# A hybrid decoder layer on one core: fp32 side products spread between dense passes, and an opening loaded and ordered differently

## The reference

```python
xn = rms_norm(h, pre_norm[i])
proj = xn @ w_in[i]
(g_q, g_k, g_v, g_a, g_z, n_q, n_kc, n_vc, n_ks, n_vs, n_kw, n_vw, n_g, n_z) = \
    jnp.split(proj, SPLIT_POINTS, axis=-1)
log_a = jax.nn.log_sigmoid((g_a @ gla_a_up[i] + gla_a_bias[i]).astype(jnp.float32)) / GLA_TAU
o_gla = gla_mixer(g_q..., g_k..., g_v..., log_a...)
...
    flat = blocks.transpose(0, 1, 3, 2, 4).reshape(B, n_cmp, NSA_KV_HEADS, CMP_LEN * NSA_DH)
    return jax.nn.silu(flat @ w1) @ w2        # compressed keys and values of the NSA
...
mixed = jnp.concatenate([o_gla, o_nsa], axis=-1) @ w_out[i]
h = h + rms_norm(mixed, post_norm[i])
```

## Time and profile before

| | us |
|---|---|
| median of 3 runs | 894.94 |
| lowest, highest | 894.93, 896.84 |
| the profiled execution | 893.85 |
| its span, first to last instruction | 892.1 |

### The profile page before, as it was taken

The page is one execution under the profiler, slowest core; times in us unless marked ns, Lnnn a source line. Parts: engine busy times, 40 slices in busy tenths (PEclk is TensorE's granted clock), DMA queues, the critical chain, the costliest instruction groups (busy, mean ns, idle before and its releaser), DMA issues.

```text
span 892.1 us, 12441 instructions
## 1 busy us (share of the span) xinstructions
PE 840.9 (94%) x4624; PEld 693.7 (78%) x4624; DVE 538.1 (60%) x953; ACT 460.3 (52%) x928; POOL 374.0 (42%) x331
## 2 busy tenths in 40 slices
PE   6999999999999999988889998999989999999996
PEld 6878798888888788766667776777767888887884
DVE  2670449761744504666989998899966026372445
ACT  4513134223222026666879988789966252625424
POOL 3312028244221121643447655356534445463554
PEclk9999879999999999998999999999999999999999
DMA  8511011111011021310000000000007723232237
GB/s 253 134 51 48 23 33 48 48 32 52 25 48 36 24 50 49 100 36 1 1 1 1 1 1 2 1 1 1 1 1 255 240 83 98 70 110 75 98 95 247
DMA packets 38398, 55.19 MB, mean 62 GB/s; under 512 B 11313, under 2 KB 17729, under 8 KB 38338
## 3 DMA queue, kind: packets, MB, share of 16 engines
q1 hardware_dynamic: 38050, 53.35, 19.7%
q0 software_dynamic: 288, 1.05, 0.7%
HBM read 49.13 MB, written 5.25 MB: 61 GB/s over the span
## 4 chain that ended last, share of the span: by engine, by line
PE 74%; DVE 11%; ACT 10%; issue 3%; POOL 1%; DMA 0%; DVEq 0%; SPq 0%; ACTq 0%; POOLq 0%
PE psum L863 45%; PE psum L1102 3%; ACT pT_hi L1442 3%; DVE pT_lo L2042 3%; PE psum L952 3%; PE psum L1119 3%; ACT p_win L1428 2%; PE psum L1120 2%; PE psum L1086 2%; PE psum L896 2%; PE psum L1087 1%; PE psum L802 1%; PE psum L804 1%; PE psum L803 1%; DVE p_slc L2016 1%
## 5 line engine op out<-in xcount | busy, mean ns | idle before, releaser
L1563 POOL TENSOR_TENSOR w_lo<-w_raw,w_hi 128x512 fp32r<-128x512 f32 x126 | 179.9, 1431 | 353.4 <-ACT w_hi L1224 353.0
L1224 ACT ACTIVATE w_hi<-w_raw 128x512 fp32r<-128x512 f32 x126 | 79.3, 635 | 309.6 <-PE psum L863 301.3
L2042 DVE TENSOR_TENSOR pT_lo<-psum,pT_hi 128x512 fp32r<-128x512 f32 (+1 forms) x148 | 100.0, 684 | 17.2 <-ACT pT_hi L1442 16.2
L1442 ACT ACTIVATE pT_hi<-psum 128x512 fp32r<-128x512 f32 (+1 forms) x148 | 86.8, 592 | 31.8 <-PE psum L1102 30.8
L863 PE MATMUL psum<-w_hi,xT_hi 128*128 128x512 f32 x256 | 101.2, 395 | 1.7 <-DVE gla_state_b L1923 1.7
L863 PE MATMUL psum<-w_lo,xT_hi 128*128 128x512 f32 x256 | 100.1, 391 | 0.0
L863 PE MATMUL psum<-w_hi,xT_lo 128*128 128x512 f32 x256 | 100.1, 391 | 0.0
L1119 PE MATMUL psum<-pT_hi,v_hi_lo 128*128 128x512 f32 x132 | 60.9, 461 | 17.3 <-DVE pT_lo L2042 17.1
L1086 PE MATMUL psum<-kT_hi_hi,qT_hi_lo 128*128 128x384 f32 (+3 forms) x192 | 70.4, 370 | 4.3 <-DVE neg_max L2016 4.0
L1619 POOL TENSOR_SCALAR p_slc<-p_slc,gate_over_sum 128x512 f32<-128x512 f32 (+7 forms) x40 | 63.7, 1604 | 1.6
L1428 ACT ACTIVATE p_slc<-p_slc,neg_max 128x512 f32<-128x512 f32 (+7 forms) x80 | 58.1, 727 | 7.5 <-DVE neg_max L2016 7.3
(11 more groups left out here) (276 smaller groups left out, 2020.1 us busy)
## 6 DMA issues: line engine op xcount, KB each, us to landing
w_raw<-in_w_in SPq DMA_DIRECT2D x56, 256.0 KB, 2.7
w_raw<-in_w_out SPq DMA_DIRECT2D x32, 256.0 KB, 2.8
w_raw<-in_ple_gate SPq DMA_DIRECT2D x32, 256.0 KB, 2.6
x_tok<-in_x SPq DMA_DIRECT2D x8, 512.0 KB, 4.7
h_tok<-in_x SPq DMA_DIRECT2D x8, 512.0 KB, 5.0
out<-h_tok SPq DMA_DIRECT2D x6, 512.0 KB, 5.6
w_raw<-in_ple_proj SPq DMA_DIRECT2D x8, 256.0 KB, 2.5
rank_w_raw<-in_w_in SPq DMA_DIRECT2D x8, 128.0 KB, 2.8
```

The source lines that it names most:

```text
L1224: act.activation(w_hi(i)[:, 0:w], w_in(i)[:, 0:w], ACT.Copy).then_inc(s_whi, 1)
L1442: act.activation(PTh[0:n, u % 4], bank(4 + u % TRING)[0:n], ACT.Copy).then_inc(s_phi, 1)
L1563: pool.tensor_tensor(w_lo(i)[:, 0:w], w_in(i)[:, 0:w], w_hi(i)[:, 0:w].bitcast(F32), ALU.subtract).then_inc(s_wlo, 1)
L2042: dve.tensor_tensor(PTl[0:n, u % 4], bank(4 + u % TRING)[0:n], PTh[0:n, u % 4].bitcast(F32), ALU.subtract).then_inc(s_plo, 1)
```

## The change

It does six things. (1) PE runs four fp32 products of 256 columns on constants before the first transposes and three behind them (`keep_busy`); nobody reads them. (2) ACT loads its function table with a tiny copy right after the constants. (3) The rank weights come in nine transfers (slice 0, slices 1 to 3, slices 4 to 7), all ahead of tiles 2 to 7 of x; the rank-up weights and bias follow x. (4) In group 0 the transposes of tiles 2 and 3 stand behind slices 4, 5, 6 and 7. (5) Two of the four rank-up products run inside group 2, behind its slice 6, the other two between hidden products 6 and 12. (6) The diagonals stream 64 columns (the same two, repeated) and stand, with the compression's output, between the banks of the first pass of `gv`, whose bank order is 0, 1, 2, 3, 6, 4, 5, 7. DVE and the waits follow suit.

```diff
 CUTS = ((0, 48), (48, 176), (176, 304))
+LOADS = ((0, 1), (1, 4), (4, 8))
 LEVELS = (2, 4, 8, 16, 32, 64, 128)
...
         if i < KD:
-            eng.wait_ge(s_ag[i], 48)
+            eng.wait_ge(s_ag[[lo <= i < hi for lo, hi in LOADS].index(True)], 48)
         else:
...
-        def load_rank_piece(k):
-            rows, dst, w = slice(k * P, (k + 1) * P), AGR[:, k], a["w_in"][0]
-            sp.dma_start(dst[:, 0:32], w[rows, NG_:NG_ + 32]).then_inc(s_ag[k], 16)
-            sp.dma_start(dst[:, 32:48], w[rows, GA:GA + RANK]).then_inc(s_ag[k], 16)
-            sp.dma_start(dst[:, 48:304], w[rows, NKC:NKC + 256]).then_inc(s_ag[k], 16)
+        def load_rank_pieces(n):
+            lo, hi = LOADS[n]
+            rows, w = slice(lo * P, hi * P), a["w_in"][0]
+            for at, col, size in ((0, NG_, 32), (32, GA, RANK), (48, NKC, 256)):
+                sp.dma_start(AGR[:, lo:hi, at:at + size],
+                             w[rows, col:col + size].rearrange("(k p) c -> p k c", p=P)).then_inc(s_ag[n], 16)
...
         load_x(1)
-        for k in range(3):
-            load_rank_piece(k)
-        load_x(2)
-        load_x(3)
-        for k in range(3, KD):
-            load_rank_piece(k)
-        for t in range(4, NT):
+        for n in range(len(LOADS)):
+            load_rank_pieces(n)
+        for t in range(2, NT):
             load_x(t)
+        sp.dma_start(GAU[32:32 + RANK, :], a["gla_a_up"][0]).then_inc(s_gau, 16)
+        sp.dma_start(GBI[:], a["gla_a_bias"][0].rearrange("(c p) -> p c", p=P),
+                     allow_slow_non_contiguous=True).then_inc(s_gau, 16)
         for i in range(KD, KD + RAW):
...
                          allow_slow_non_contiguous=True).then_inc(s_small, 16)
-        sp.dma_start(GAU[32:32 + RANK, :], a["gla_a_up"][0]).then_inc(s_small, 16)
-        sp.dma_start(GBI[:], a["gla_a_bias"][0].rearrange("(c p) -> p c", p=P),
-                     allow_slow_non_contiguous=True).then_inc(s_small, 16)
         sp.dma_start(GGN[:], a["gla_out_norm"][0].partition_broadcast(P)).then_inc(s_small, 16)
...
+        def rank_up(half, ct):
+
+            pe.matmul(bank(2 * half + ct), GAU[32:32 + RANK, ct * P:(ct + 1) * P],
+                      AG[32:32 + RANK, half * 512:half * 512 + 512],
+                      start=True, stop=True).then_inc(s_la, 1)
+
+        def keep_busy(n):
+
+            for _ in range(n):
+                pe.matmul(bank(0)[:, 0:256], ident, CT[:, 0:256], start=True, stop=True)
+
+        keep_busy(4)
         for t in range(2):
...
                     mm.then_inc(s_xtr, 1)
+        keep_busy(3)
         for k in range(KD):
             project_rank(0, k)
-            if 2 <= k < 6:
-                turn_x(4 + k - 2)
+            if k >= 4:
+                turn_x(k)
         for k in range(KD):
...
                               DR[:, half].rearrange("p t j -> p (t j)"), start=True, stop=True).then_inc(s_rrow, 1)
-
-        def project(name, tokens, ready=None, begin=0):
+            if k == 6:
+                pe.wait_ge(s_gau, 32)
+                for ct in range(2):
+                    wait_read(pe, cidx["ag"], ct)
+                    rank_up(0, ct)
+
+        def project(name, tokens, ready=None, begin=0, first_order=None, between={}):
...
                     if first:
-                        b = (b + begin) % banks
+                        b = first_order[b] if first_order else (b + begin) % banks
                     if first and ready:
...
                         mm.then_inc(s_bank, 1)
+                    if first and b in between:
+                        between[b]()
                 if not final:
...
                 pe.wait_ge(s_rt, b - 5)
+            elif b < 2:
+                pe.wait_ge(s_z, b + 1)
             else:
...
-
-        pe.wait_ge(s_small, 16 * 39)
-        for ct in range(2):
-            for half in range(2):
-                wait_read(pe, cidx["gqk"], ct * 2 + half)
-                pe.matmul(bank(ct * 2 + half), GAU[32:32 + RANK, ct * P:(ct + 1) * P],
-                          AG[32:32 + RANK, half * 512:half * 512 + 512],
-                          start=True, stop=True).then_inc(s_la, 1)
+        def hidden(n, l):
+
+            flat = DC[:, n].rearrange("p c t -> p (c t)")
+            blocks = flat[:, 2 * l:2 * l + CSTR * (CROWS - 1) + 1:CSTR]
+            return pe.matmul(bank(4 + n)[:, 0:CROWS], W1[:, n, l], blocks, start=(l == 0), stop=(l == 15))
+
+        def diagonal(t):
+
+            if t == 0:
+                pe.wait_ge(s_cbr, 1)
+                pe.wait_ge(s_prod, 1)
+            for ct in range(2):
+                at = t * GH + 2 * ct
+                mm = pe.matmul(bank(7)[:, at:at + 64], QKP[:, ct, t * P:(t + 1) * P],
+                               CT[:, C_HEAD:C_HEAD + 2].unsqueeze(1).to_broadcast([P, 32, 2]), start=True, stop=True)
+            if t == NT - 1:
+                mm.then_inc(s_diag, 1)
+
+        def compressed():
+
+            pe.wait_ge(s_ch, 1)
+            for n in range(2):
+                for kv in range(NKV):
+                    mm = pe.matmul(bank(4 + n)[0:NCMP, kv * DH:(kv + 1) * DH], HCT[:, n, kv * 64:kv * 64 + NCMP],
+                                   W2[:, n], start=True, stop=True)
+            mm.then_inc(s_cout, 1)
+
+
+        pe.wait_ge(s_small, 16 * 37)
         pe.wait_ge(s_dcs, 2)
-        for n in range(2):
-            wait_read(pe, cidx["gqk"], 4 + n)
-            for l in range(16):
-
-                flat = DC[:, n].rearrange("p c t -> p (c t)")
-                blocks = flat[:, 2 * l:2 * l + CSTR * (CROWS - 1) + 1:CSTR]
-                mm = pe.matmul(bank(4 + n)[:, 0:CROWS], W1[:, n, l], blocks, start=(l == 0), stop=(l == 15))
+        wait_read(pe, cidx["gqk"], 4)
+        for l in range(16):
+            hidden(0, l)
+            if l in (5, 11):
+                wait_read(pe, cidx["gqk"], 2 + l // 11)
+                rank_up(1, l // 11)
+        wait_read(pe, cidx["gqk"], 7)
+        for l in range(16):
+            mm = hidden(1, l)
+            if l == 2:
+                pe.wait_ge(s_pws, 2)
+                for n in range(2):
+                    m1 = pe.matmul(bank(7)[:, n:n + 1], PS_[:, n], CT[:, C_ONE:C_ONE + 1], start=True, stop=True)
+                m1.then_inc(s_cb, 1)
         mm.then_inc(s_cmp, 1)
-        wait_read(pe, cidx["gqk"], 7)
-        pe.wait_ge(s_pws, 2)
-        for n in range(2):
-            mm = pe.matmul(bank(7)[:, n:n + 1], PS_[:, n], CT[:, C_ONE:C_ONE + 1], start=True, stop=True)
-        mm.then_inc(s_cb, 1)
-        wait_read(pe, cidx["gqk"], 6)
         pe.wait_ge(s_agg, 1)
...
         mm.then_inc(s_gtr, 1)
-        pe.wait_ge(s_cbr, 1)
-        pe.wait_ge(s_prod, 1)
-        for t in range(NT):
-            for ct in range(2):
-                mm = pe.matmul(bank(7)[:, t * GH + 2 * ct:t * GH + 2 * ct + 2], QKP[:, ct, t * P:(t + 1) * P],
-                               CT[:, C_HEAD:C_HEAD + 2], start=True, stop=True)
-        mm.then_inc(s_diag, 1)
-        pe.wait_ge(s_ch, 1)
-        for n in range(2):
-            for kv in range(NKV):
-                mm = pe.matmul(bank(4 + n)[0:NCMP, kv * DH:(kv + 1) * DH], HCT[:, n, kv * 64:kv * 64 + NCMP], W2[:, n],
-                               start=True, stop=True)
-        mm.then_inc(s_cout, 1)
...
-            if b < 4:
-                pe.wait_ge(s_z, 4)
+            if b < 2:
+                wait_read(pe, cidx["gqk"], b)
+            elif b < 4:
+                pe.wait_ge(s_z, b + 1)
             elif b < 6:
...
                 pe.wait_ge(s_dg, 1)
+
+        def diagonals(b):
+            def some():
+                for t in {0: (0,), 1: (1,), 2: (2,), 3: (3, 4), 6: (5, 6, 7)}[b]:
+                    diagonal(t)
+                if b == 2:
+                    compressed()
+            return some
...
-        project("gv", xt, after_compression)
+        project("gv", xt, after_compression, first_order=(0, 1, 2, 3, 6, 4, 5, 7),
+                between={b: diagonals(b) for b in (0, 1, 2, 3, 6)})
         for lev in (0, 1, 2):
...
         act.wait_ge(s_const, 32)
+        act.activation(first_table[:], CT[:, C_ONE:C_ONE + 2], ACT.Copy)
...
-        def read_out(c):
+        def read_out(c, banks=None):
             name = chunks[c][0]
-            for b in range(chunks[c][3]):
+            for b in banks or range(chunks[c][3]):
                 ps, done = bank(b), bank0[c] + b + 1
...
-        def raise_rank(ct):
-
-            for half in range(2):
-                dve.wait_ge(s_la, 2 * ct + half + 1)
-                dve.tensor_scalar(GLZ[:, ct, half * 512:half * 512 + 512], bank(2 * ct + half),
+        def raise_rank(half):
+
+            for ct in range(2):
+                dve.wait_ge(s_la, 2 * half + ct + 1)
+                dve.tensor_scalar(GLZ[:, ct, half * 512:half * 512 + 512], bank(2 * half + ct),
                                   GBI[:, ct:ct + 1], None, ALU.add).then_inc(s_z, 1)
...
         dve.wait_ge(s_xtr, 2 * KD)
-        read_out(cidx["ag"])
```

(6 more changed lines are left out.)

4 lines of the change are left out of this document (3 added, 1 removed).

## The result

The changed kernel takes 900.32 us (median of 5 runs, 899.01 to 901.10); the kernel before took 894.93 beside it (892.90 to 896.84). The ratio is 1.006 with an interval of 1.0042 to 1.0078: slower by 0.6%. The forecast was 902.2 within 897.6 to 906.5, slower. The profiled execution took 901.1 us with a span of 899.3; before, and all others come from a span of 892.1.

What follows compares the result with a forecast made beforehand. PE was taken to bound the kernel. Group 1 5.8 us later (pauses 7.2 less slow clock 1.4), plus 3.0 for the clock, less 1.5 for the stage, gives +7.3 on 894.94: 902.2 us, range 897.6 to 906.5.

Steps and rivals of the forecast that it cites:

- first product: Start of group 0: first rank product at 11.5 us against 11.46, between 10.7 and 12.3; start and table load cancel.
- slow clock of the first slices: Group 0: the first slices run at 2.4 GHz instead of about 1.2, which gives back 1.4 us.
- three pauses: Group 0: PE stands 2.40 us before each of slices 5, 6 and 7, waiting for ACT and POOL; 7.2 us.
- clock in the pauses: Group 0 into group 1: PE's clock falls in the pauses and costs 3.0 us, between 0 and 4.5.
- stage behind gqk: Between gqk and gv: gains 2.9 us, less 1.0 for a new wait and 0.4 for product changes; 1.5 us net.
- The two cases: Start: first product at 12.0 or 12.3 us with transposes at 1.2 GHz, 10.7 or 10.4 with the clock up.
- a diagonal's price: Between gqk and gv: 0.21 us per diagonal is its weight load; 64 columns hide under it, higher clock gains nothing.
- Rival D: Not slower: clock at 2.4 GHz through gv's first pass, early start, stage gives its full 2.9 us; 897.1 us, chance 0.11.
- much more than 3 us: Sign that the prediction is wrong: the stage behind gqk gives back much more than 3 us.
- A: The forecast: three pauses in group 0, clock falls in them, short products keep it up later; 902.2 us, chance 0.52.
- B: The pauses in group 0 come, but the clock outlasts them; 899.2 us, chance 0.22.
- C: The clock falls a second time, in gv's first pass, which runs partly slow; 905.3 us, chance 0.15.

Runs made afterwards that it cites:

- as_is: The changed kernel once more, unedited, for a second profile: 900.14 us, ratio 1.0062.
- act_order: The changed kernel with ACT making the high parts of slices 4 to 7 before it takes up transpose units 4 to 7: 892.78 us, ratio 0.998.
- turns_back: The changed kernel with the transposes of tiles 2 and 3 put back behind slices 2 to 5 of group 0: 890.58 us, ratio 0.9971.
- turns_only: The kernel before with only the transposes of tiles 2 and 3 moved behind slices 4 to 7 of group 0: 906.1 us, ratio 1.0135.
- filled: The changed kernel with four constant fp32 products of 256 columns put into each of the three pauses: 899.91 us, ratio 1.006.
- no_busy: `act_order` without the seven constant products, early table load kept: 892.81 us, ratio 0.9984.
- early_diag: `act_order` with the diagonals moved ahead, two token tiles behind each of banks 0 to 3: 891.83 us, ratio 0.9963.
- best: `early_diag` with three constant products ahead of the transposes and two behind, instead of four and three: 890.39 us, ratio 0.9954.
- block64: The kernel before with diagonals streaming 64 columns instead of 2, in the old single block: 893.98 us, ratio 0.9989.
- before_again: The kernel before once more, unedited, for a second profile: 895.2 us, ratio 1.0016.
- cols2: `act_order` with diagonals of 2 columns instead of 64, at the same spread places: 892.03 us, ratio 0.9973.
- stage_only: The changed kernel with the opening of the kernel before, so only the stage between gqk and gv stays changed: 893.48 us, ratio 0.9997.

## Why the prediction was right, and where it was not

The time was 1.9 us from the forecast (+5.4 against +7.3), the sign and the chief cause were right. By its own sum, for the two profiles of the changed kernel (the price of the slow clock at the start is what is left over in the column of `as_is`; the prices of the fall and of the stage are worked out above):

| term | forecast | first profile | `as_is` |
|---|---|---|---|
| first product | 0 | −0.9 | −0.4 |
| slow clock of the first slices | −1.4 | −1.4 | −1.4 |
| three pauses | +7.2 | +7.3 | +7.3 |
| clock in the pauses | +3.0 | +2.0 | 0 |
| stage behind gqk | −1.5 | −3.7 | −2.3 |
| attention stages | 0 | +3.9 | +1.8 |
| sum | +7.3 | +7.2 | +5.0 |

**The pauses** were the step that decides, and every part of it held: the place, the chain of ACT and POOL, 2.40 us forecast and 2.43 measured for each, 7.3 in all. `act_order` and `turns_back` take them away in two different ways, and by the ratios 7 to 8 us go with them (1.006 becomes 0.998 and 0.9971); `turns_only` brings them into the kernel before alone. `filled` confirms the sum to 0.1 us where the clock has no part: −0.93 − 1.4 + 7.3 = 4.97, and group 2 stood at +4.95.

**The clock in the pauses** was mis-sized: 2.0 us where it falls, not 3.0, and it doesn't always fall. The rule of the Trainium skill (TensorE: Matmul & The Clock Gate, Why this matters for your kernels) that pauses between bursts have to be longer than these before they matter would have excluded it. One profile agrees with the rule and one doesn't: in the first it fell at 23.9 us, at the beginning of the third pause of 2.18 us.

**The start.** My value was 11.5 us, between 10.7 and 12.3; 10.52 and 11.04 were measured, and 10.46 to 11.25 in the experiments with all seven constant products, so the early bound was too late as well. Sixteen transposes took some 2 us, not 3.65, because the constant products had brought the clock up by 6.8 to 8.1 us. The two cases had been written down; the choice of the middle was the error. That the constant products would also hide a late tile of x wasn't seen. Slice 0 at 1.09 us confirms the clock's part, and `no_busy`, 1.6 us later than `act_order` at group 2 with the same first product, is near its 1.4; on the median it doesn't show.

**The stage behind gqk** is where a step failed. The prediction held that a diagonal's price is its weight load of 0.206 us "although the clock was low", so that "the higher clock gains nothing". It took 0.21 us from the timeline at 1.2 GHz and 0.206 from the record of another line's weight loads at 2.4 GHz, and called them one. The weight loads of the diagonals themselves would have told: in the kernel before they are 333 ns long at 1.2 GHz, at a distance of 0.21, so the record's length isn't the distance and goes with the clock. So would the block's own first matmuls, 0.11 us apart at 116.56 and 116.67 us, ahead of the fall.

```profile
L912 PEld LDWEIGHTS psum<-consts,gla_qk_products x23: 333/333/333, 117.2 to 121.9; 128*128 128x128 f32 x23
```

The same line after, 128.2 to 130.9 us, with the clock at 2.4 GHz, min, median and max in ns:

```profile
L916 PEld LDWEIGHTS psum<-consts,gla_qk_products x19: 187/192/192, 128.2 to 130.9; 128*128 128x128 f32 x19
```

The diagonals and the compression's output took 124.13 − 116.43 = 7.70 us before and 4.85 after with the wait in it, so a gain of 2.85 where −1.0 was forecast (0 for them and the wait of 1.0, which was 0.79). The other terms were smaller than forecast: the dense products of `gv`'s first pass gained 0.8, not 1.1 (1.5 less the 0.4 for the changes between product kinds), as each switch from a diagonal to a dense product costs some 0.1 us (0.32 to the next start instead of 0.23); the rank product 0.3 instead of 1.0, in the best case (with a fall in the hidden layer it is a loss of 0.6); the hidden layer lost 0.2 instead of gaining 0.4. Together 3.7 instead of 1.5. Rival D had asked for 2.9 as the most that this stage could give, and the prediction named "much more than 3 us" as a sign that it is wrong. With 3.7 in one profile and 2.3 in the other that sign wasn't clearly reached; the step on the diagonals' price was wrong all the same.

**The attention stages** had no term at all. In the first profile they took 3.9 us more, in the second 1.8, though nothing is changed there. In the profiles that show it, `turns_only`, `no_busy` and the first of the change, the fall of the clock ahead of the compressed keys lasts 6.8 us instead of 3.4 and costs 1.35 to 1.45 us; and those with a fall between 641 and 658 us (both of the change, `turns_only`, `early_diag`, `no_busy` and `best`) lose 1.2 to 1.8 there, the others 0.03 to 0.34. `act_order` had neither and won 1.4. So the losses go with the clock's falls; what decides in which execution they come, and whether a kernel that is shifted by some us has them more often, stays open. The medians leave room for it: of the changed kernel's 5.4 us (0.006 × 895) the shift at GLA explains 3.2, and in all other kernels but `block64` too the ratio stands 1.1 to 3.5 us above the shift at GLA. As `before_again`, with nothing changed, is one of them (+1.4 against +0.3), part of this is how the profiled executions fell.

So the forecast came near in part by luck: 2.2 us too little gain in the stage and 3.9 us of loss that it didn't know of nearly cancelled. In the second profile the fall that didn't come, 3.0 us too much, was in part made up by a loss of 1.8.

**Rivals.** A happened in the first profile and B in the second, with B's 899.2 one us below the measured medians. C, a fall in `gv`'s first pass, didn't happen in any of the ten profiles with the spread diagonals. D was out. For faster outright the prediction gives 0.05 in one place and 0.04 in another; nothing hangs on it.

## What to carry to other kernels

Where a step is moved on one engine, look at what stands behind its consumer on the next: the transposes had to wait for nothing at their new place, but ACT had two things queued behind them that PE needed first, and one loop split in two there is worth 0.8%. The price of small matmuls has to be read as the distance from start to start, at the clock of that stretch, and for that very line; the length of a weight load record is neither a price nor a constant. And a gain under half a per cent in a kernel whose clock falls now and then needs many runs and a second profile before it is assigned to an edit: the ten runs of one kernel spread over 4 to 8 us here.

## What the hardware showed

- A real fp32 matmul of the diagonals, with 2 or with 64 columns, starts 0.11 us behind the last one at 2.4 GHz and 0.213 us at 1.2 GHz (`cols2`, `block64` and the two kernels); the two widths make no difference.
- The hidden layer doesn't follow that. Its matmuls of 127 columns, read with a stride, start 0.216 us apart in the kernel before, both at 1.2 GHz and at 2.4, in these two stretches (the counts take in matmuls that reach into a stretch; the clock is the third number from the right). So the earlier trace rows, a weight load of 206 ns, isn't the distance here either. Whether the stride is the reason wasn't tried.

```profile
101.40:106.00 4.60, 4.60 (x22) 4.60 (x22) 2.95 (x2) 1.91 (x1) 0.00 (x0) 0.50 0.00 0
107.00:115.00 8.00, 8.00 (x39) 7.61 (x38) 0.00 (x0) 0.00 (x0) 0.00 (x0) 1.00 0.00 0
```

- The clock fell in or just ahead of that hidden layer in every profile but the first of the change, although PE's row has no gap there, and at three pauses of 2.18 us it fell in one execution and not in the next. In two of the six profiles without the constant products, `stage_only` and `turns_only`, the record has the clock down from 12.5 to 16.0 and from 12.3 to 15.8 us; in the others it has no fall in the opening. With the same program the time moves by up to 7.6 us (`block64`: 889.69 to 897.26, with a mean clock of 0.988 and 0.978), and the mean clock doesn't always follow it (`act_order`: 893.42 us at 0.988, 892.64 at 0.984).
- The early table load sits at 0.73 us, ahead of the arrival of the constants, where ACT has nothing else to do. The arrival of the constants themselves (3.5 to 4.2 us) and of tile 0 of x (5.35 to 6.67) differ between executions by 0.7 and 1.3 us.
